# Two transformer blocks in one kernel: where the forget-gate products, copies, additions and last products of the second block stand in the queues

## The reference, cut to what matters

```python
def _hgrn_scan(q, k, v, lf, S):            # gated linear attention, forget gate per channel
    # per chunk: b = cumsum(lf); a[t,s] = sum_k q[t,k] exp(b[t,k]-b[s,k]) k[s,k], s <= t
    # o = a @ v + (q * exp(b)) @ S;  S = exp(b_last) * S + (k * exp(b_last - b))^T v
def _mlstm_scan(q, k, v, ig, lf, state):   # scalar gates per token, running maximum mt
    # s = (q k^T) * exp(dlog - mt);  h = (s @ v + inter) / max(|den|, exp(-mt))
...
pl = _modulate(_rmsnorm(xl, norm1_w), sh1, sc1) @ w_in     # latent: q, two z (forward, backward), v, g; mLSTM q, k, v, o
pc = _modulate(_rmsnorm(xc, norm1_w), sh1c, sc1c) @ w_in   # context
hg: lf = log(lb + (1-lb) sigmoid(z)), k = (1-lb) sigmoid(-z), for both directions
ml: q, k = silu(dwconv2d(p)), both directions of the scan are added
xl = xl + g1 * (concat([ml, hg]) @ w_out)
u = dwconv2d(_modulate(_rmsnorm(xl, norm2_w), sh2, sc2) @ w_up)   # 5632 channels, 8 x 64 image, 9 taps
a, b = split(u); xl = xl + g2 * ((silu(a) * b) @ w_down)
return _rmsnorm(xl, final_norm_w)
```

## Time and profile before

| | |
|---|---|
| median of 3 runs | 1814.64 us (1813.74 to 1817.5) |
| the profiled execution | 1816.16 us, its span 1814.4 us |
| TensorE busy | 1715.5 us (95%) |
| VectorE busy | 1181.8 us (65%) |
| ScalarE busy | 730.6 us (40%) |
| GpSimd busy | 458.5 us (25%) |
| mean granted clock of TensorE | 0.972 of full |
| mixer rounds, 1070 to 1425 us | TensorE busy 333.6 of 355 |
| feed-forward part, 1445 to 1769 us | TensorE busy 324.0 of 324 |
| from 1769 to 1814 us | TensorE busy 30.8 of 45 |

### The profile page before, as it was taken

One profiled execution on the slowest core, in us unless ns is written; L12 is line 12 of the kernel. 1 busy time (PEld: TensorE's weight loads), 2 busy tenths in 40 slices (PEclk: granted clock), 3 DMA queues, 4 the chain that ended last, 5 costly groups with the idle time before them and its releaser, 6 DMA issues.

```text
span 1814.4 us, 21556 instructions
## 1 busy us (share of the span) xinstructions
PE 1715.5 (95%) x7645; PEld 1311.3 (72%) x7645; DVE 1181.8 (65%) x2193; ACT 730.6 (40%) x1176; POOL 458.5 (25%) x448
## 2 busy tenths in 40 slices
PE   7998897999997999999999989999999899999996
PEld 3456654578885888888867877878757588888885
DVE  5977654353446765577566366878884687777776
ACT  3164456442353321232144436547462443233324
POOL 2831200030020110011000113232330266556452
PEclk9999789999998999999999999999999899999999
DMA  6254110043333554455422212111311332423311
GB/s 153 70 109 127 47 47 1 18 127 100 103 116 105 174 185 139 131 174 188 140 85 60 70 31 62 47 47 48 116 36 47 116 116 79 131 70 116 93 47 47
DMA packets 185537, 168.69 MB, mean 93 GB/s; under 512 B 17639, under 2 KB 168867, under 8 KB 185051
## 3 DMA queue, kind: packets, MB, share of 16 engines
q1 hardware_dynamic: 173083, 128.19, 23.2%
q0 software_dynamic: 11808, 39.29, 7.3%
q10 hardware_dynamic: 560, 0.12, 0.0%
HBM read 155.83 MB, written 6.31 MB: 89 GB/s over the span
## 4 chain that ended last, share of the span: by engine, by line
PE 80%; DVE 9%; ACT 6%; issue 3%; POOL 1%; DMA 1%; POOLq 0%; DVEq 0%; SPq 0%; ACTq 0%
PE bank L1510 28%; PE bank L1929 18%; PE bank L1621 4%; PE bank L1815 3%; DVE arena L2681 2%; PE bank L1303 2%; PE bank L1670 2%; PE bank L1626 2%; PE bank L1463 2%; PE bank L1449 2%; PE bank L1405 1%; PE bank L1807 1%; PE bank L1729 1%; PE bank L1766 1%; PE bank L1661 1%
## 5 line engine op out<-in xcount | busy, mean ns | idle before, releaser
L3597 DVE SCALAR_TENSOR_TENSOR arena<-bank,ffn_taps,arena 128x441 f32<-128x441 f32 (+2 forms) x352 | 220.1, 685 | 79.4 <-ACT arena L2641 79.4
L3052 DVE TENSOR_TENSOR w_lo<-ring,w_hi 128x2048 fp32r<-128x2048 f32 x52 | 119.2, 2292 | 117.1 <-ACT w_hi L2214 113.3
L1510 PE MATMUL bank<-h_lo,w_hi 128*128 128x512 f32 x448 | 176.5, 394 | 3.2 <-DVE w_lo L3052 1.8
L2214 ACT CAST w_hi<-ring 128x2048 fp32r<-128x2048 f32 x52 | 99.1, 1906 | 176.5 <-PE bank L1510 176.5
L1510 PE MATMUL bank<-hT_hi,w_hi 128*128 128x512 f32 x384 | 153.5, 400 | 6.6 <-DVE h_lo L3138 5.9
L1161 POOL TENSOR_TENSOR w_lo<-ring,w_hi 128x2048 fp32r<-128x2048 f32 x21 | 99.6, 4745 | 165.0 <-ACT w_hi L2614 165.0
L1510 PE MATMUL bank<-act_hi,w_hi 128*128 128x512 f32 x352 | 137.9, 392 | 0.2
L1510 PE MATMUL bank<-act_lo,w_hi 128*128 128x512 f32 x352 | 131.8, 389 | 0.0
L1929 PE MATMUL bank<-hT_hi,w_hi 128*128 128x512 f32 x336 | 130.8, 389 | 0.3 <-POOL w_lo L1161 0.3
L1929 PE MATMUL bank<-hT_hi,w_lo 128*128 128x512 f32 x336 | 130.7, 389 | 0.0
L1929 PE MATMUL bank<-h_lo,w_hi 128*128 128x512 f32 x336 | 130.7, 389 | 0.0
(11 more groups left out here) (577 smaller groups left out, 4013.3 us busy)
## 6 DMA issues: line engine op xcount, KB each, us to landing
ring<-in_w_up SPq DMA_DIRECT2D x76, 512.0 KB, 4.5
arena<-in_w_mod POOLq DMA_DIRECT2D x48, 512.0 KB, 4.2
ring<-in_w_in SPq DMA_DIRECT2D x72, 256.0 KB, 3.0
ring<-in_w_down SPq DMA_DIRECT2D x32, 512.0 KB, 4.2
ring<-in_w_in SPq DMA_DIRECT2D x30, 512.0 KB, 3.9
arena<-in_w_down SPq DMA_DIRECT2D x22, 512.0 KB, 4.4
ring<-in_w_out SPq DMA_DIRECT2D x8, 512.0 KB, 3.9
ring<-in_w_out SPq DMA_DIRECT2D x16, 256.0 KB, 3.0
```

Source lines behind the costliest of these rows:

```text
L1510: ins = pe.matmul(out, u[:, n % SLOTS, cols], v[:, k, :], start=start and k == w[0][0] and m == 0, stop=stop and k == w[-1][0] and m == 2)
L2214: sc.copy(w_hi[:, n % SLOTS, :], ring[:, n % SLOTS, :]).then_inc(hi_ready, 1)
L3052: ve.tensor_tensor(w_lo[:, n % SLOTS, :], ring[:, n % SLOTS, :], value(w_hi[:, n % SLOTS, :]), ALU.subtract)\
L3597: return ve.scalar_tensor_tensor(o[:, ys, xs], x[:, yt, xt], ffn_taps[:, at:at + 1], o[:, ys, xs], ALU.mult, ALU.add)
```

## The change

Four things are moved; nothing is computed otherwise.

1. Round 0: zf of head 1 goes behind unit 0 and zb behind unit 1, as in rounds 1 and 2, for tiles, TensorE, ScalarE's cast and VectorE's split. With it EARLY ends at mlk0, so that zf1 and zb1 use the pairs of slots, and mlq0 and mlk0 go to half slots 1 and 2 in place of 3 and 0.
2. ScalarE at positions 3 and 4: the copies of HALVES come ahead of silu of q and mlq's cast; the second six mLSTM weights go from position 3 to the end of position 4.
3. Round 3: VectorE adds a tile A ahead of its gaps, no longer behind them.
4. Feed-forward part, last tile: both up products come ahead of the remaining down products; VectorE does all taps of the first half and then those of the second half with the sums between them; split of the last down weights ahead of the last gate.

```diff
@@ mixer_tiles
-    def decays(kind, i): ...
+    tile("first", "zf", 0); tile("ml", "zc", 0); tile("first", "zb", 0)
...
-    decays("dense", 1)
...
             if n == 0:
+                tile("dense", *(("zf", i + 1) if more else ("A", 0)))
                 if i:
-                    tile("dense", *(("zf", i + 1) if more else ("A", 0)))
                     tile("o", "o", i - 1)
-            if n == 1 and i:
+            if n == 1:
@@ places of the chunks
-EARLY = CHUNK_AT["zb1"] + 1
+EARLY = CHUNK_AT["mlk0"] + 1
-            raw.append(n % WEIGHTS)
+            raw.append({"mlq0": 1, "mlk0": 2}.get(name, n % WEIGHTS))
@@ GpSimd and ScalarE, feed-forward part (down_low on the one, down_high on the other)
+                if j == F2T:
+                    down_low(DOWNS - 1)
                 if j:
                     gate(j - 1)
-                if j % 2 == 0 and j:
+                if j % 2 == 0 and 0 < j < F2T:
                     down_low(j // 2 - 1)
@@ TensorE, mixer
-            decay_in(1, 0)
-            decay_context(1, 0)
-            decay_last(1)
...
-                    if n == 0 and i:
+                    if n == 0:
                         if more:
                             decay_in(i + 1, 0)
                             decay_context(i + 1, 0)
...
-                    if n == 1 and more and i:
+                    if n == 1 and more:
                         decay_last(i + 1)
@@ TensorE, feed-forward part
-                    if j >= 4:
+                    if 4 <= j < F2T - 1:
                         for c in range(2):
                             down(j // 2 - 2, j % 2 * 4 + m * 2 + c)
+            for c in range(4):
+                down(DOWNS - 3, 4 + c)
@@ ScalarE, mixer
-            mix_high("zb1")
...
-                        if i and more:
+                        if more:
                             mix_high(f"zb{i + 1}")
...
                     if n == 3:
                         ml_weights(i, 0)
                         mix_high(f"g{i}")
-                        ml_weights(i, 1)
                     if n == 4:
+                        weights(i, HALVES, a_half[:, 0:2], a_half[:, 2:4])
                         if more:
                             silu(hg_q[:, (i + 1) % 2, :], "q", i + 1)
                             mix_high(f"mlq{i + 1}")
-                        weights(i, HALVES, a_half[:, 0:2], a_half[:, 2:4])
...
                         if i:
                             tail_roots()
+                        ml_weights(i, 1)
@@ VectorE, mixer
-            mix_low("zb1")
...
-                    if n == 1 and i and more:
+                    if n == 1 and more:
                         mix_low(f"zb{i + 1}")
...
+                    if n in (1, 2, 3, 4, 6, 7) and not more:
+                        out_add("A", n - 1 if n < 5 else n - 2)
                     if n in (1, 2):
                         ml_gaps(i, n - 1)
...
-                    if n in (1, 2, 3, 4, 6, 7) and not more:
-                        out_add("A", n - 1 if n < 5 else n - 2)
@@ VectorE, feed-forward part
-            for j in range(F2T):
+            for j in range(F2T - 1):
...
+            for m in range(2):
+                before = None
+                for n, k in enumerate(around):
+                    ins = tap(F2T - 1, m, k, before)
+                    if n == len(around) - 1:
+                        out_of(T0["up2"] + 2 * (F2T - 1) + m, ins)
+                    else:
+                        before = step.mark(ins)
+                    if m and n % 2:
+                        residual2(DOWNS - 3, 4 + n // 2)
```

More of the change, by code:

```diff
@@ L136, in tile @@
         plan.append((key, places[turn[kind] % len(places)]))
[L138 to L141, removed]
     for b in range(CT):
@@ L148, in mixer_tiles @@
         tile("first", "v", 0, b)
-    decays("first", 0)
+    tile("first", "zf", 0)
+    tile("ml", "zc", 0)
+    tile("first", "zb", 0)
     tile("first", "q", 0)
@@ L1879, in _ @@
                             out_first(0)
-                        hg_outputs(i - 1)
-                    if n == 1 and more and i:
+                        if i:
+                            hg_outputs(i - 1)
+                    if n == 1 and more:
                         decay_last(i + 1)
@@ L2657, in _ @@
                     up_high(j + 2)
+                if j == F2T:
+                    down_high(DOWNS - 1)
                 if j:
                     gate(j - 1)
-                if j % 2 == 0 and j:
+                if j % 2 == 0 and 0 < j < F2T:
                     down_high(j // 2 - 1)
```

## The result

| | before | after |
|---|---|---|
| median of the runs | 1814.19 us (1812.8 to 1817.5, 4 runs) | 1799.74 us (1799.23 to 1800.0, 4 runs) |
| ratio | | 0.9911, 95% interval 0.9899 to 0.9924 |
| the profiled execution, its span | 1816.16, 1814.4 us | 1799.23, 1797.5 us |
| TensorE busy, mean granted clock | 1715.5 us, 0.972 | 1710.7 us, 0.975 |

The change is faster by 14.5 us in the medians and by 16.9 us between the two profiled spans. The ratio on record is the estimate from all executions and not the quotient of the two medians (0.9920); by itself it stands for 16.1 us, its interval for 13.8 to 18.3. The forecast was 24.0 us, to 1790.6, with a range of 1786.5 to 1799.5. The measured median lies 0.2 beyond the slow end of that range; by the ratio, taken of the 1814.64 that the forecast started from, it would be 1.0 inside.

A forecast was written before the change was run, and what follows sets the result against it. TensorE, busy in 95% of the span, was taken as the bound, so only its holes and lower clock could give time. Gains 8.4 + 8.6 + 4.2 + 2.8 = 24.0 us led from 1814.64 to 1790.6, range 1786.5 to 1799.5.

The forecast's parts named there:

- The reasoning on units 0 and 1: Round 0: units 0 and 1 ahead of zf1 and zb1 let ScalarE and VectorE work under 16.8 us of products.
- Added: the weights of mlq0: Round 0: mlq0's weights load later in their new half slot, so its product is late; a cost of 1.2 us.
- The 0.6 for unit 0 behind mlk0's copy: Round 0: unit 0 takes mlk0's bank and waits for ScalarE's copy of it; a cost of 0.6 us.
- What is late next: Rounds 1 and 2: mlk's cast would end at 1190.9, with TensorE there at 1191.0, so no new wait.
- ScalarE takes over: Rival, 17%: ScalarE's queue is 1.5 us longer in each of three rounds, making mlk's cast late; time 1795.1.
- The 0.3 for mlq's cast: Rounds 1 and 2: mlq's cast ends at 1180.2, unit 5 at 1179.9; a new wait of 0.3 us a round.
- The 1.6 in each of rounds 1 and 2: Rounds 1 and 2: sixteen products behind unit 5's wait return to full clock, 3.73 us instead of 5.28; a gain.
- the 2.0 in round 3: Round 3: eight products behind the removed wait run at full clock, 3.43 us instead of 5.40; a gain.
- The wait's own term: Round 3: A2's wait of 3.4 us goes, and a new wait of 1.2 us for unit 3's factors comes.
- the clock's (1800.0): Rival, 8%: new waits of 1.2, 0.6 and 1.2 us start spells of lower clock; time 1800.0.
- round 0 gives little: Rival, 12%: round 0's wait and lower clock come back behind unit 2 or q1, 8.4 becomes 0; time 1799.0.
- Slower: Rival, 4%: ScalarE's queue in position 4 sets each round's length, 30 us lost against 24.0; time 1821.

The follow-up runs named there:

- the old slot: The changed kernel with mlq0's weights back in half slot 3, as in the kernel before, in place of 1: 1797.41 us.
- The copy-first kernel: The changed kernel with ScalarE's copy of mlq's bank ahead of mlk's cast and unit 8's factors: 1797.06 us.
- three edits: The changed kernel with mlq0's weights in half slot 3, mlq's copy ahead of mlk's cast, and the six weights at the end of position 5: 1791.66 us.
- part 1's: The kernel before with only the round 0 moves (forget gates behind units 0 and 1, new half slots for mlq0 and mlk0): 1811.75 us.
- parts 1, 3 and 4: Three kernels, each the kernel before with only that numbered item of the change: 1811.75, 1812.69 and 1813.01 us.
- part 4's like mixer: The kernel before with only the last tile's feed-forward moves, its mixer unchanged: 1813.01 us.
- in turn: The changed kernel with VectorE's sixteen taps of the last tile taken from both halves alternately, as before the change: 1796.63 us.
- parts 1 and 2: The kernel before with only the round 0 moves, 1811.75 us; with only ScalarE's reordering at positions 3 and 4, 1811.07 us; with both, 1806.89 us.
- the six weights on ScalarE: The changed kernel with the second six mLSTM weights back at position 3, ahead of HALVES' factors and copies: 1804.92 us.

## Why the forecast was right in direction and too high

- **Round 0: 8.4 forecast, 5.6 measured** (8.13 less 2.55). The reasoning on units 0 and 1 held: in after no wait over 0.54 us and full clock from 1066 to 1098. Too small was "Added: the weights of mlq0", charged at 1.2: it cost 2.55, a wait of 0.96 and 1.6 of clock, which the old slot gives back whole. The 0.6 for unit 0 behind mlk0's copy was 0.7. With 1.35 for mlq0, 0.97 for the copy of the next point and 0.3 more for mlq1's cast, 2.6 of the 2.8 are named.
- **Rounds 1 and 2: 4.3 each forecast, 2.7 and 2.6 measured.** This is the main error. "What is late next" named mlk's cast and found "It just fits". It did, by 0.4 us. But the product waits for a bank as well as for a cast, and the copy that frees it stands two factors behind the cast on ScalarE, 1.5 us later. The prediction names the cast alone and no bank for this product. The copy-first kernel gives back 0.97, 0.98 and 0.7 in rounds 0 to 2. With the six weights behind that cast as well (three edits), round 1 takes 79.72, 4.2 less than before: the 4.3 was there to be had, behind the copy (1.0) and the weights (0.5). The rival "ScalarE takes over" had the right engine and lost 1.5 a round, for a reason that was not the one measured: its queue was not longer than counted (the cast was to end at 1190.9; it ended at 1185.76 in a round that began 5.12 earlier, 1190.88), one of its customers was left out. The 0.3 for mlq's cast was 0.5.
- **Clock.** The 1.6 in each of rounds 1 and 2 and the 2.0 in round 3 were read from one execution. Round 1's stretch was there in all four profiles with that 3.0 us wait (3.4 us long in three of them, 6.8 in part 1's). Round 2's was in one of four (r2 is 83.3 to 83.7 in parts 1, 3 and 4, against 85.15), round 3's in three of five. So about 3 us of the 16.9 between the profiles were the luck of the profiled execution. That may be part of why the medians differ by 14.5; which stretches the other executions had is not on record.
- **Round 3: 4.2 forecast, 2.8 measured.** A2 began right behind its neighbour unit, and HALVES waited 1.38 for its factors, forecast 1.2. TensorE's and VectorE's rows:

```profile
1316.47 3.70 PE L1813 MATMUL bank<-arena,ring 128*128 128x512 f32 x8
1321.54 1.97 PE L1731 MATMUL bank<-root,sq 128*128 128x256 f32 x8 [1.38 <-DVE root L3388]
```

```profile
1316.34 3.79 DVE L3425 TENSOR_SCALAR arena<-arena 128x512 f32<-128x512 f32 x6
1320.71 0.68 DVE L3388 SCALAR_TENSOR_TENSOR root<-root,arena 128x512 f32<-128x512 f32 x1
```

  The wait's own term was 3.36 less 1.38, 2.0 and not 2.2. The clock's was too large as well: before took 112.79 with it and part 4's like mixer 111.44 without, with 0.2 more in its wait for L3459 (1.05 against 0.86), so some 1.5 and not 2.0. The changed kernel has that 0.2 too. This makes 3.3, and 0.5 stays unexplained.
- **Last stage: 2.8 forecast, 3.7 measured.** The sums came 2.0 apart, as forecast (1758.87, 1760.89 above), the split and the last gate stayed hidden (no wait for L1167 is left). Counted from the first up product, the taps began 0.7 us earlier than forecast, and the five products took 1.36 each, not 1.43.
- **The rivals.** Two rivals named this figure nearly, the clock's (1800.0) and "round 0 gives little" (1799.0), and both by luck. Round 0 gave 5.6 and not nothing. As for the clock, of the new waits only that for mlq0 had the lower clock behind it, those of 1.2, 0.7 and 1.4 us in no profile. The rule of the Trainium skill behind it (TensorE: Matmul & The Clock Gate, section A second HAM failure mode: psum-queue depth-cycling), read as the prediction reads it, would have had the clock swing behind these waits, and the trace does not agree. "Slower" and "nothing" are excluded by the time.
- **Chains on VectorE.** The taps in a chain took 0.71 each, near the 0.72 of the earlier trace rows, and 0.64 in turn. So a tap that waits for the one just before it costs 0.07 more. By the Trainium skill (VectorE: DVE Perf Modes, section The DRAIN you can't avoid), which measured it on eight copies, the semaphore between them would cost nothing; for this chain the trace does not agree. It decided nothing, since the start of the taps gave back what their rate lost.
- **The signs.** Neither of the two signs of being wrong came: no wait over 2 us in rounds 0 to 3, and one stretch of lower clock in the mixer. Yet some 9.5 us of 24 were missing: waits of 1.2 us, one a round, and a mis-sized clock pass under such signs. Of the signs of being right one failed and points at the cause: mlk's cast was to lie within 1 us of its product, and in round 1 it ended 1.5 us ahead.

## What to carry to other kernels

When a wait on one engine goes, list for the next product everything it waits for (its weights' cast, its factors, the release of its bank) and take the latest; a cast that just fits says nothing if the copy that frees the bank is queued behind it. Where a change is worth 1 to 3 us, compare waits and stages between marks on the engine that bounds, and not medians alone. But a stage with a stretch of lower clock in it is one draw: parts 1 and 2 gave 1.4 and 1.5 us over round 0 in their profiles and 5.5 together, and that gap, mostly clock, isn't seen in the means of six to eleven executions. Look at several executions before counting the clock as part of a wait's price.

## What the runs showed of the hardware

- The lower clock does not go by the length of the wait alone. The wait for mlq0's cast (0.96 us in the changed kernel, 0.9 to 1.1 in the others), right behind 1.39 us of twenty 4x4 products, was followed by 3.4 us at the lower level in all seven profiles that have it; the seven that don't have the wait have full clock there. Waits of 1.2 and 1.4 us in rounds 0 to 3 had it in none, those of 2.3 us (the six weights on ScalarE) in one of three, 3.0 us in round 2 in one of four. What TensorE did before the wait seems to matter; that was not tested by itself.
- A lower-clock stretch of 3.4 us cost its stage 1.35 to 1.95 us, by the stages of like code with it and without: r3 112.79, 113.36 and 113.39 against 111.44 and 111.46, r2 85.15 against 83.30 to 83.66. At half speed 3.4 us cost at most 1.7, so the upper figures hold something else too.
